# RWKV core of a diffusion block: the 16x16 diagonal blocks inverted on GpSimd, two levels of doubling on TensorE, and the next pair's triangles made behind them

## The reference, cut to what matters

```python
def step(s, inp):
    r_t, w_t, k_t, v_t, a_t, b_t = inp
    sa = jnp.einsum('dbhvk,dbhk->dbhv', s, a_t)
    s = s * w_t[..., None, :] + sa[..., :, None] * b_t[..., None, :] + v_t[..., :, None] * k_t[..., None, :]
    return s, jnp.einsum('dbhvk,dbhk->dbhv', s, r_t)
s_final, y = lax.scan(step, s0, (r, w, k, v, a, b))
```

## Time and profile before

| | us |
|---|---|
| median of 3 timed runs | 3311.89 (3311.46 to 3314.42) |
| profiled execution, its own time | 3313.88 |
| its span | 3312.1 |
| TensorE busy | 3099.8 (94%) |
| VectorE, ScalarE, GpSimd busy | 1567.8, 733.2, 1058.2 |
| first inverse of the core begins | 1092.3 |
| last x of its last pair's z and w | 1630 |

### The profile page before, as it was taken

How to read it: one execution, slowest core, us unless ns; L and a number is a source line. 1 busy time by engine, 2 the same in 40 slices (tenths; PEclk the granted TensorE clock), 3 DMA queues, 4 the chain that set the end, 5 groups by cost and what they waited for, 6 DMA issues and landing times.

```text
span 3312.1 us, 70246 instructions
## 1 busy us (share of the span) xinstructions
PE 3099.8 (94%) x30244; PEld 2572.7 (78%) x30244; DVE 1567.8 (47%) x1977; ACT 733.2 (22%) x1079; POOL 1058.2 (32%) x482
## 2 busy tenths in 40 slices
PE   6799997999995999999999899999999999999996
PEld 0577885788784999999888688888888888888885
DVE  0667667446785445545432733333433333333336
ACT  0322222012222222222111322212121212222221
POOL 0343343443430000000034344444444444444442
PEclk7799997999997999999999999999999999999998
DMA  9665566322333111110242122222222222222222
GB/s 405 228 221 203 200 230 233 100 79 101 131 122 151 50 44 50 50 50 21 88 191 95 66 94 96 96 96 96 96 95 96 96 93 94 94 95 96 96 96 108
DMA packets 103203, 392.69 MB, mean 119 GB/s; under 512 B 15104, under 2 KB 16896, under 8 KB 96128
## 3 DMA queue, kind: packets, MB, share of 16 engines
q1 hardware_dynamic: 72288, 289.43, 24.8%
q10 hardware_dynamic: 30336, 96.64, 8.3%
q0 software_dynamic: 288, 2.10, 0.2%
HBM read 355.87 MB, written 32.26 MB: 117 GB/s over the span
## 4 chain that ended last, share of the span: by engine, by line
PE 64%; DVE 2%; issue 1%; ACT 0%; POOL 0%; ACTq 0%; DVEq 0%; POOLq 0%
PE bank L931 16%; PE bank L932 16%; PE bank L930 16%; PE bank L671 12%; PE bank L687 2%; PE bank L747 1%; PE bank L735 1%; PE bank L815 1%; PE bank L813 1%; DVE buf L1793 0%; DVE buf L1794 0%; PE bank L695 0%; DVE buf L1510 0%; DVE buf L1750 0%; PE bank L759 0%
## 5 line engine op out<-in xcount | busy, mean ns | idle before, releaser
L514 POOL TENSOR_TENSOR buf<-buf 128x1024 fp32r<-128x1024 f32 x288 | 697.2, 2421 | 1581.1 <-ACT buf L1130 1581.1
L931 PE MATMUL bank<-buf 128*128 128x512 f32 x2304 | 909.6, 395 | 0.0
L932 PE MATMUL bank<-buf 128*128 128x512 f32 x2304 | 908.0, 394 | 0.0
L930 PE MATMUL bank<-buf 128*128 128x512 f32 x2304 | 903.4, 392 | 0.5 <-POOL buf L514 0.3
L1130 ACT CAST buf<-buf 128x1024 fp32r<-128x1024 f32 x288 | 302.7, 1051 | 1263.8 <-PE bank L932 1261.8
L930 PEld LDWEIGHTS bank<-buf 128*128 128x128 f32 x2304 | 433.0, 188 | 104.4 <-issue 1.9
L931 PEld LDWEIGHTS bank<-buf 128*128 128x128 f32 x2304 | 432.5, 188 | 101.4 <-issue 0.5
L932 PEld LDWEIGHTS bank<-buf 128*128 128x128 f32 x2304 | 432.6, 188 | 95.7
L671 PE MATMUL bank<-buf 64*64 64x64 f32 x13248 | 430.6, 220 | 26.4 <-issue 13.9
L538 PE MATMUL bank<-buf 128*128 128x512 f32 (+1 forms) x1168 | 431.7, 370 | 21.3 <-POOL buf L508 14.2
L671 PEld LDWEIGHTS bank<-buf 64*64 64x64 f32 x13248 | 413.8, 137 | 38.7 <-issue 34.3
(11 more groups left out here) (214 smaller groups left out, 2380.0 us busy)
## 6 DMA issues: line engine op xcount, KB each, us to landing
buf<-stream SPq DMA_DIRECT2D x382, 512.0 KB, 3.3
buf<-adarows ACTq DMA_DIRECT2D x108, 512.0 KB, 5.1
buf<-ada SPq DMA_DIRECT2D x32, 1024.0 KB, 13.0
scaled_keys<-buf ACTq DMA_DIRECT2D x18, 768.0 KB, 5.8
buf<-scaled_keys SPq DMA_DIRECT2D x18, 768.0 KB, 7.0
buf<-adarows SPq DMA_DIRECT2D x20, 512.0 KB, 6.9
buf<-tokens SPq DMA_DIRECT2D x4, 1536.0 KB, 21.1
buf<-bias ACTq DMA_DIRECT2D x6, 1024.0 KB, 6.2
```

Of the source, the lines that this page charges most:

```text
L514: G.tensor_tensor(wl2[b % SPLIT2], raw2[b], wh2[b % SPLIT2].bitcast(F32), ALU.subtract).then_inc(split2, 1)
L930: pe.matmul(bank[:, :], lh, rh, start=start, stop=False)
L931: pe.matmul(bank[:, :], lh, rl, start=False, stop=False)
L932: return pe.matmul(bank[:, :], ll, rh, start=False, stop=stop)
```

## The change

The doubling keeps two levels, 16 and 32. The 16x16 diagonal blocks are inverted on GpSimd: the triangles of both directions are stored to DRAM (`gather`), the 4 diagonal blocks of each of the 24 matrices of a direction come back as 96 partitions of 256 elements for each of two directions (Y), GpSimd sets the diagonals to one, does 14 times a multiply and an add on the trailing rows, and a transposed copy (YT). `scatter` writes Y and YT into the diagonal blocks of two images of the full matrices in DRAM, whose other elements are zero since the start, and `load_inverses` loads X and XT from there in eight transfers. SP's order per pair is now gather and block loads, AH, BH, KH and values of the next pair, scatter, X and XT, receptances of the next pair, bonus and gates (`late`).

lowT and low leave `front` and become `lows`, five banks made right behind the levels of the pair before (low only for the first direction, into LG). LT has two buffers. Three of the ten chain steps stand between those banks, the other seven beside the levels; `read` and `mean` of the pair before move between the z and w groups, and its variance into `front`. ScalarE's filling of X and XT is gone. The masks shrink by six, TR moves, and two of the last outputs' tiles lie over it.

```diff
-LEVELS = [2, 4, 8, 16, 32]
+LEVELS = [16, 32]
+BASE = 16
...
+CHAIN_BESIDE_LOWS = {1: 8, 2: 9, 4: 10}
+VARIANCE_BEHIND = 5
...
+        PITCH = T * T + T
+        lowd = nc.dram_tensor("lower_triangles", (2, 2 * NC * PITCH), F32, kind="Internal").ap()
+        ximg, xtimg = (nc.dram_tensor(f"inverse_image_{d}", (2, 2 * NC * PITCH), F32, kind="Internal").ap() for d in range(2))
...
+            def load_vectors(j):
                 if j:
-                    ready(sp, ("low", j - 1, 2))
+                    ready(sp, ("tA", j - 1, 2), ("rk", j - 1, 1))
+                sp.wait_ge(F["hst"], 64 * (j + 1))
+                sp.wait_ge(F["ost"], 16 * (j + 1))
+                sp.dma_start(AH, hatd[j, 0]).then_inc(R["ab"], 16)
+                sp.dma_start(BH, hatd[j, 1]).then_inc(R["ab"], 16)
+                sp.dma_start(KH, hatd[j, 2]).then_inc(R["load"], 16)
+                sp.dma_start(cV, valued[j, :, 0:TOK]).then_inc(R["load"], 16)
+
+            def load_receptances(j):
                 if j > 1:
                     ready(sp, ("rc", j - 2, 1))
-                sp.wait_ge(F["hst"], 64 * (j + 1))
-                sp.wait_ge(F["ost"], 16 * (j + 1))
-                for n, dst in enumerate((AH, BH, KH)):
-                    sp.dma_start(dst, hatd[j, n]).then_inc(R["load"], 16)
-                sp.dma_start(cV, valued[j, :, 0:TOK]).then_inc(R["load"], 16)
                 sp.dma_start(RH[j % 2], readd[j]).then_inc(R["load"], 16)
+
+            def load_late(j):
                 if j == 1:
                     sp.wait_ge(F["hst"], 64 * BPAIRS)
                     sp.wait_ge(F["ost"], 16 * BPAIRS)
                 if j > 1:
                     sp.wait_ge(R["done"], j - 1)
                 sp.dma_start(late[j % 2], valued[j, :, TOK:]).then_inc(R["late"], 16)
+
+            def matrices(a, d, h):
+
+                return a[d].rearrange("(c h e) -> c h e", h=2, e=PITCH)[:, h, 0:T * T].rearrange("c (r s) -> r c s", s=T)
+
+            def blocks(a, d):
+
+                return a[d].rearrange("(b e) -> b e", e=BASE * (T + 1))[:, 0:BASE * T].rearrange("b (r s) -> b r s", s=T)[:, :, 0:BASE]
+
+            def packed(a, d):
+                return a[0:8 * NC, BASE * BASE * d:BASE * BASE * (d + 1)].rearrange("p (r s) -> p r s", r=BASE)
+
+            def half(a, d, h):
+                return both_dirs(a)[T * h:T * h + T, :, d, :]
+
+            def gather(j):
+                ready(sp, ("lowT", j, 0), ("lowT", j, 1), ("lowT", j, 2), ("low", j, 0), ("low", j, 1))
+                for h in range(2):
+                    sp.dma_start(matrices(lowd, 0, h), chunks(LG)[T * h:T * h + T]).then_inc(R["lg"], 16)
+                    sp.dma_start(matrices(lowd, 1, h), half(LT[j % 2], 1, h)).then_inc(R["lg"], 16)
+                sp.wait_ge(R["lg"], 64 * (j + 1))
+                for d in range(2):
+                    sp.dma_start(packed(Y, d), blocks(lowd, d)).then_inc(R["yl"], 16)
+
+            def scatter(j):
+                sp.wait_ge(R["sub"], 1 + SUB_STEPS * (j + 1))
+                sp.wait_ge(R["img"], 128 + 64 * j)
+                sp.wait_ge(R["xl"], 128 * j)
+                for d in range(2):
+                    sp.dma_start(blocks(ximg, d), packed(YT if d else Y, d)).then_inc(R["img"], 16)
+                    sp.dma_start(blocks(xtimg, d), packed(Y if d else YT, d)).then_inc(R["img"], 16)
+
+            def load_inverses(j):
+                sp.wait_ge(R["img"], 128 + 64 * (j + 1))
+                if j:
+                    ready(sp, ("inv", j - 1, NX - 1))
+                for d in range(2):
+                    for h in range(2):
+                        sp.dma_start(half(X, d, h), matrices(ximg, d, h)).then_inc(R["xl"], 16)
+                if j:
+                    ready(sp, ("z", j - 1, 2), ("w", j - 1, 2))
+                for d in range(2):
+                    for h in range(2):
+                        sp.dma_start(half(XT, d, h), matrices(xtimg, d, h)).then_inc(R["xl"], 16)
+
+            load_vectors(0)
+            load_receptances(0)
+            load_late(0)
+            sp.wait_ge(R["sub"], 1)
+            for d in range(2):
+                for h in range(2):
+                    sp.dma_start(matrices(ximg, d, h), half(X, d, h)).then_inc(R["img"], 16)
+                    sp.dma_start(matrices(xtimg, d, h), half(X, d, h)).then_inc(R["img"], 16)
+            gather(0)
+            load_vectors(1)
+            scatter(0)
+            load_inverses(0)
+            load_receptances(1)
+            for j in range(1, BPAIRS):
+                gather(j)
+                if j + 1 < BPAIRS:
+                    load_vectors(j + 1)
+                scatter(j)
+                load_inverses(j)
+                if j + 1 < BPAIRS:
+                    load_receptances(j + 1)
+                load_late(j)
...
+            pool.wait_ge(used1, N1)
+            step(G.memset(X, 0.0))
+            a = Y[0:96, :].rearrange("p (h r s) -> p h r s", h=2, r=BASE)
+            at = YT[0:96, :].rearrange("p (h r s) -> p h r s", h=2, r=BASE)
+            for j in range(BPAIRS):
+                pool.wait_ge(R["yl"], 32 * (j + 1))
+                step(G.memset(Y[0:96, :].rearrange("p (h e) -> p h e", h=2)[:, :, 0:BASE * BASE:BASE + 1], 1.0))
+                for k in range(1, BASE - 1):
+                    rows, shape = BASE - 1 - k, [96, 2, BASE - 1 - k, k]
+                    part = product[0:96, 0:2 * rows * k].rearrange("p (h r s) -> p h r s", h=2, r=rows)
+                    step(G.tensor_tensor(part, a[:, :, k + 1:, k:k + 1].to_broadcast(shape), a[:, :, k:k + 1, 0:k].to_broadcast(shape), ALU.mult))
+                    step(G.tensor_tensor(a[:, :, k + 1:, 0:k], a[:, :, k + 1:, 0:k], part, ALU.add))
+                step(G.tensor_copy(at.rearrange("p h r s -> p h s r"), a))
...
+            def lows(j, n):
+
+                pe.wait_ge(R["ab"], 32 * (j + 1))
+                if n < 3:
+                    blocks(("lowT", j, n), BH, AH, n)
+                else:
+                    key = ("low", j, n - 3)
+                    bank = fill(key)
+                    for i in range(8 if n == 3 else 4):
+                        for hs in heads:
+                            mm = pe.matmul(bank[hs, T * i:T * i + T], AH[hs, inst(8 * (n - 3) + i, 0)], BH[hs, inst(8 * (n - 3) + i, 0)],
+                                           start=True, stop=True)
+                    mm.then_inc(full(key), 1)
...
-                        ready(pe, ("invX", j, x - 3) if l else ("low", j, g))
-                        if l == 0:
-                            ready(pe, ("lowT", j, g))
-                        blocks(("inv", j, x), LT, X, g)
+                        ready(pe, ("invX", j, x - 3) if l else ("lowT", j, g))
+                        if x == 0:
+                            pe.wait_ge(R["xl"], 128 * (j + 1))
+                        blocks(("inv", j, x), LT[j % 2], X, g)
...
-                    if j and 1 <= x < NC - 1:
-                        chain(j - 1, x)
-                    if j and x == NC:
-                        read(j - 1)
-                    if j and x == NC + 2:
-                        mean(j - 1)
+                    if j:
+                        chain(j - 1, 1 + x)
...
+                for n in range(5):
+                    if j + 1 < BPAIRS:
+                        lows(j + 1, n)
+                    if j and n in CHAIN_BESIDE_LOWS:
+                        chain(j - 1, CHAIN_BESIDE_LOWS[n])
                 for g in range(3):
                     ready(pe, ("invT", j, NX - 3 + g), ("gv", j, g), ("tA", j, g))
                     blocks(("z", j, g), XT, GV, g)
                     blocks(("w", j, g), XT, AT, g)
-                if j:
+                    if j and g == 0:
+                        read(j - 1)
+                    if j and g == 1:
+                        mean(j - 1)
+                if j + 1 < BPAIRS:
+                    front(j + 1, j - 1 if j else None)
+                elif j:
...
-            def start_inverse(j):
-
-                if j:
-                    act.wait_ge(filled[USES[("w", j - 1, 2)][0]], USES[("w", j - 1, 2)][1])
-                units = eye[:, None, :].to_broadcast([P, NI, T])
-                nc.scalar.copy(X.rearrange("p (u n) -> p u n", n=T), units).then_inc(R["xi"], 1)
-                nc.scalar.copy(XT.rearrange("p (u n) -> p u n", n=T), units).then_inc(R["xi"], 1)
```

More of the change, by code:

```diff
@@ L12 @@
+import itertools
 from contextlib import ExitStack
@@ L109, in bank_uses, with front @@
     add = lambda key, bank, reader: order.append((key, bank, reader))
-    def front(j):
-        for (name, g), bank, reader in TURN_GRAM:
+    def front(j, out=None):
+        for n, ((name, g), bank, reader) in enumerate(TURN_GRAM):
             add((name, j, g), bank, reader)
+            if out is not None and n == VARIANCE_BEHIND:
+                add(("var", out), 6, "s")
     def values(j):
@@ L311, in build_block @@
         RH.append(fc(NL * T))
-        AT, GV, TT, XT, X, LT = (fc(NI * T) for _ in range(6))
```

(37 more changed lines are left out.)

132 lines of the change are left out of this document (80 added, 52 removed).

## The result

| | median us (range, runs) | ratio to before (95%) |
|---|---|---|
| before | 3311.68 (3308.74 to 3314.42, 4) | |
| after | 3227.53 (3219.84 to 3229.34, 4) | 0.9745 (0.9732 to 0.9759) |

The change makes the kernel 84 us faster, where I had said 50. The profiled execution took 3225.99 us, span 3224.2, against 3313.88 and 3312.1.

A forecast was written before the change was run, and what follows sets the result against it. TensorE was taken as the bound, with the new transfers and GpSimd steps setting the changed period. +30 for pair 0, -58.5 for five periods and -22 at the end gave -50: 3262 us, own range 3232 to 3292, wide range 3205 to 3395.

The forecast's parts named there:

- A: From the start of a pair's first inverse product through the next pair's triangles, with clock loss after the wait: 24.5 us.
- vectors' gate: SP's loads of the next pair's vectors wait for tA ahead of the scatter and hold it some 9 us.
- B: After the triangles, TensorE's 43.5 us beside the transfers and GpSimd, 60.5 us; TensorE stands for 17 us.
- Work saved: Block products per pair: 28.5 fewer groups of 0.93 us, 26.5 us less TensorE; some 1250 matmuls for 2220.
- Rival 4: Transfers and GpSimd are covered and TensorE stays the bound: period 70, -140 us, 3172; chance 2%.
- Short runs: DRAM transfers of triangles, blocks and inverses: 1.2 ns per 64 B run, 1.6 ns per 256 B run.
- rival 2: Scatter and block loads run at a slow 3.8 ns per 64 B run: period 105.5, +80 us, 3392; chance 24%.
- GpSimd: Inversion of the diagonal blocks: 28 steps plus unit diagonal and turn, 16 us per pair (12 to 37).
- Pair 0: The first pair has no cover: its first inverse product moves from 1092.3 to 1122, +30 us.
- the period is 85 us ... 5 x -11.7: All five periods between pairs fall from 96.7 to 85 us, 11.7 less each, -58.5 together.
- After the last start: Behind the last pair's start: 27 groups less, -25.1, and 3 for the clock, -22 us.
- Rival 1: Short runs at 0.7 and 1.2 ns, GpSimd 13 us: period 79, -92 us, 3220; chance 17%.

The follow-up runs named there:

- experiment 1: Kernel after, with the next pair's AH, BH, KH and values issued behind the scatter and the loads of X and XT: 3189.32 us, ratio 0.9637.
- experiment 2: 18 more small GpSimd products per pair: 3238.16 us in the kernel after, 3231.32 us in the version with the vectors' loads behind X and XT.
- the run without the path: Kernel after, with triangle stores, block loads, GpSimd steps, scatters and X and XT loads left out for pairs 1 to 5: 3173.02 us, ratio 0.9576.

## Why the prediction was right in kind and 34 us off

One gated period by the prediction's terms, from the rows above (inverse product 1265.80 to the next at 1348.45):

| step | predicted us | measured us |
|---|---|---|
| A, to the stores | 24.5 | 24.3 |
| stores to block loads | 7.3 | 7.0 |
| block loads to GpSimd | 6.1 | 4.1 |
| GpSimd | 16 | 12.9 |
| vectors' gate, from the stores | 31.5 | 31.1 |
| from the gate to the loads of X, XT | 16.5 | 15.5 |
| loads of X and XT | 12.2 | 11.8 |
| B | 60.5 | 58.3 |
| period | 85 | 82.7 |

- *The wait*: 10 to 12 us where I had said 17, though B is only 2 us shorter. In the period above TensorE's own work in B took 46 us (58.3 less a wait of 12.3) and not 43.5; a pause of 2.0 us at 1331.05 is in it.
- *Work saved*: the group is still 0.93 us; 1256 products of blocks in a period where the earlier trace rows had 2220, as predicted (some 1250). Rival 4's price of the kernel without the path's cost, 3172, came out as a total in the run without the path, 3173.
- *The gate*: right for pairs 2 to 4, shown by experiment 1 and, from the other side, by experiment 2, where 9.5 us more of GpSimd cost these periods nothing.
- *Short runs*: lower bound right (0.7), the value taken from it, 1.2, too high for the 0.6 to 0.9 ns measured. In a gated period the scatter shares the engines with 2.7 MB of vectors (15.5 us together, 16.5 predicted), so the cheaper runs gained 1 us there. The "DMA: Bandwidth & Descriptors" page of the Trainium skill (specifications) has a read-modify-write below 512 B, which stood behind rival 2; whatever the engine does, 6144 writes of 64 B cost 3.9 us here, a quarter of what that rival needed (2.6 ns a run).
- *GpSimd*: 28 steps at 0.415 us from start to start (11.61 / 28) where I had 0.52. Between 28 and 112 elements the time goes from 0.24 to 0.41 us, so 2.0 ns an element and 0.18 us of start-up. The multiply, which reads a column whose rows lie 64 B apart, and the add take the same (0.41, 0.40): the half more of the Trainium skill's "GPSIMD Engine Reference" (performance pitfalls) doesn't show here. But the column is broadcast along the innermost dimension, so its 64 B are not the innermost step, and no run here tests that rule.
- *Pair 0*: predicted +30 from 1092.3. What starts at 1092.28 is not the first inverse product but the first of the three groups of `values`, which the kernel puts between `front` and `inverse`. ScalarE's copies of these products are spaced 0.93 us and begin at 1093.46, and the fourth belongs to the first inverse product, which starts 1.18 us ahead of it, at 1095.1. The fourth copies of pairs 0, 1 and 5:

```profile
1096.27 0.59 ACT L1135 COPY buf<-bank 128x512 f32<-128x512 f32 x1 [0.35 <-PE bank L671]
...
1182.91 0.59 ACT L1135 COPY buf<-bank 128x512 f32<-128x512 f32 x1 [0.35 <-PE bank L671]
...
1568.76 0.59 ACT L1135 COPY buf<-bank 128x512 f32<-128x512 f32 x1 [0.35 <-PE bank L671]
```

  So the predicted 1122 is +27, and the measured 1113.17 is +18.1 (20.3 from the core on), by the same terms without a gate.
- *The failed step is "the period is 85 us ... 5 x -11.7"*. I worked out one gated period against one of 96.7 and used the difference for all five. By these copies and those between them the kernel before took 86.6, 96.7, 96.7, 96.7 and 95.7 us from first inverse product to first inverse product, 472.5 in all and not 483.5; the kernel after took 70.7, 82.0, 82.7, 81.3 and 71.2, 387.8 in all and not 425. The gains are 16.0, 14.7, 14.0, 15.4 and 24.6, together 84.7 where I had 58.5. The two ends differ in kind. Between pair 0 and 1 there is no chain, read or mean beside the path, in either kernel. The last pair has no next pair, so SP has no vectors ahead of its scatter, nothing is gated, and it gains 24.6. Of the 26 us that I had too little, 13 are the last period's, 4 the first's and 9 those of the three gated ones.
- *After the last start*: predicted -22. From the last pair's first inverse product to the first load of the last stage's streamed weights with all three of its parts it takes 63.1 us in the kernel before (1567.6 to 1630.67) and 42.0 in the one after (1500.94 to 1542.94): -21.1.
- *The sum*: 18.1 - 84.7 - 21.1 = -87.7, which is the -87.9 of the profiled executions but for 0.2; the prediction's 30 - 58.5 - 22 = -50.5.
- *Rival 1 came nearer*: 3220 with 17%, against 3262 with 48%. Its terms were the better ones: GpSimd 13 (12.9 measured), runs at the lower end, +18 for pair 0 (+18.1). Its period of 79 was not: the three gated ones took 81 to 83, since the scatter behind the gate took 15.5 us and not 13.5 and the loads of X and XT 11.8 and not 9.5. That its five periods (-88) still come near the measured -84.7 is luck, made by the last one.
- *My own range* had 5 us of path each way for six pairs. It had no term for pairs to which the mechanism does not apply.

## What to carry to other kernels

Work out the period of a steady pair, and then the first and the last one each by its own queue, in the kernel before as well as in the changed one: what gates the middle may not exist at the ends, and with six pairs the last period alone gave 25 of the 88 us. When a small critical transfer and a large uncritical one share a queue, put the small one first; here that order alone was worth 38 us. And a pause of TensorE marked "issue" some 4 to 6 us behind a burst of loads is a hint to spread them: the kernel before gained 13 us by waiting between four of them.

## What was not expected of the hardware

- TensorE pauses for 2 to 3 us behind a burst of loads of which it needs none yet; behind pauses of 2.35, 2.68 and 2.88 us the clock is at 0.50 to 0.74 for 2 to 4 us, behind one of 2.06 (to 1380.49 in the kernel before) it stays at 1.00. With the loads spread, the same pauses last 1 to 2 us.
- SP's own issue of a scatter of 1536 runs takes 0.3 to 1.6 us on a quiet queue and up to 3.8 behind 2.7 MB of loads in the period above (1327.86), 4.9 in the next; all that stands behind it in SP's queue goes out that much later.
- Extra products ahead of a wait kept the clock at 1.00 where 2.59 us stayed idle, and did not where 3.15, 3.54 or 5.78 did.
